# Normalised mLSTM heads turned by VectorE and two DMAs instead of TensorE

## What is computed

```python
num = jnp.einsum('bhts,bhsd->bhtd', s, v) + inter[..., None] * jnp.einsum('bhvd,bhtd->bhtv', C, q)
den = jnp.sum(s, axis=-1) + inter * jnp.einsum('bhd,bhtd->bht', n, q)
h = num / jnp.maximum(jnp.abs(den), jnp.exp(-m_t))[..., None]
...
hm = hm * lax.rsqrt(jnp.mean(hm * hm, axis=-1, keepdims=True) + EPS)
mlstm_out = hm.reshape(B, S, D_MLSTM) * mh_norm_g[l] * o_gate * jax.nn.silu(z_mlstm)
mix = jnp.concatenate([pool_out, mlstm_out], axis=-1)
x = x + gate[:, None, :] * (mix @ w_out[l])
```

## Time and profile before

| | us |
|---|---|
| time, median of 3 runs (1849.15 to 1852.01) | 1849.21 |
| the profiled execution, its own time | 1848.88 |
| its span in the profile | 1847.1 |
| PE busy | 1809.6 |
| VectorE busy | 1013.3 |
| ScalarE busy | 521.5 |

### The profile page before, as it was taken

How to read it: one execution, slowest core, us unless ns; L and a number is a source line. 1 busy time by engine, 2 the same in 40 slices (tenths; PEclk the granted TensorE clock), 3 DMA queues, 4 the chain that set the end, 5 groups by cost and what they waited for, 6 DMA issues and landing times.

```text
span 1847.1 us, 25117 instructions
## 1 busy us (share of the span) xinstructions
PE 1809.6 (98%) x9537; PEld 1554.0 (84%) x9537; DVE 1013.3 (55%) x2247; ACT 521.5 (28%) x1054; POOL 262.1 (14%) x229
## 2 busy tenths in 40 slices
PE   6989999999999999999999999999999999999998
PEld 5878889888898888988888888888889888898886
DVE  6685684527736276353863357452673627735383
ACT  3344331332323132222222223132222313222221
POOL 3433222040210003000030001200022000300000
PEclk9899999999999999999999999999999999999999
DMA  9896735595256552665427653466535665266431
GB/s 329 272 313 181 239 116 181 165 327 194 93 189 194 191 186 85 211 203 178 155 91 242 203 193 104 163 204 216 179 99 189 187 198 189 78 212 202 150 124 69
DMA packets 144348, 336.85 MB, mean 182 GB/s; under 512 B 13068, under 2 KB 55012, under 8 KB 144228
## 3 DMA queue, kind: packets, MB, share of 16 engines
q1 hardware_dynamic: 129028, 312.56, 50.9%
q10 hardware_dynamic: 15200, 22.68, 4.1%
HBM read 288.86 MB, written 46.33 MB: 181 GB/s over the span
## 4 chain that ended last, share of the span: by engine, by line
PE 88%; DVE 7%; issue 2%; ACT 1%; DMA 1%; SPq 0%; POOL 0%; ACTq 0%; DVEq 0%; POOLq 0%
PE ps_acc L511 23%; PE ps_acc L513 23%; PE ps_acc L512 23%; PE ps_kv L511 2%; PE ps_kv L512 2%; PE ps_kv L513 2%; PE ps_num L728 1%; PE ps_kv L732 1%; PE ps_num L727 1%; PE ps_sco L708 1%; PE ps_num L524 1%; PE ps_num L511 1%; PE ps_num L513 1%; PE ps_num L512 1%; PE ps_bro L740 1%
## 5 line engine op out<-in xcount | busy, mean ns | idle before, releaser
L511 PE MATMUL ps_acc<-sb_hT_hi,sb_w_split 128*128 128x512 f32 x1536 | 608.9, 396 | 0.7 <-POOL sb_w_split L1104 0.7
L513 PE MATMUL ps_acc<-sb_hT_hi,sb_w_split 128*128 128x512 f32 x1536 | 599.6, 390 | 0.0
L512 PE MATMUL ps_acc<-sb_hT_lo,sb_w_split 128*128 128x512 f32 x1536 | 598.5, 390 | 0.0
L513 PEld LDWEIGHTS ps_acc<-sb_hT_hi,sb_w_split 128*128 128x128 f32 x1536 | 288.5, 188 | 62.1
L511 PEld LDWEIGHTS ps_acc<-sb_hT_hi,sb_w_split 128*128 128x128 f32 x1536 | 289.0, 188 | 58.5 <-POOL sb_w_split L1104 0.8
L512 PEld LDWEIGHTS ps_acc<-sb_hT_lo,sb_w_split 128*128 128x128 f32 x1536 | 289.1, 188 | 56.9
L1116 POOL TENSOR_TENSOR sb_h_rs<-sb_h_var,sb_mhalf 128x4 f32<-128x4 f32 x32 | 32.4, 1013 | 1019.1 <-DVE sb_h_var L1546 1019.1
L1104 POOL TENSOR_TENSOR sb_w_split<-sb_w_raw,sb_w_split 128x512 fp32r<-128x512 f32 (+1 forms) x64 | 89.0, 1400 | 183.4 <-ACT sb_w_split L812 183.3
L1454 DVE SCALAR_TENSOR_TENSOR sb_acc_cv<-sb_shifted,sb_par,sb_acc_cv 128x512 f32<-128x512 f32 x96 | 76.9, 801 | 60.8 <-ACT sb_acc_cv L964 58.3
L1480 DVE TENSOR_TENSOR sb_oz<-sb_tanh,sb_oz 128x512 f32<-128x512 f32 x32 | 22.2, 692 | 150.5 <-ACT sb_tanh L980 150.5
L511 PE MATMUL ps_acc<-sb_wo_hi,sb_mixm_hi 128*128 128x512 f32 x256 | 103.3, 404 | 0.0
(11 more groups left out here) (219 smaller groups left out, 2867.9 us busy)
## 6 DMA issues: line engine op xcount, KB each, us to landing
sb_w_split<-w_kept SPq DMA_DIRECT2D x328, 512.0 KB, 4.0
sb_w_split<-w_kept SPq DMA_DIRECT2D x56, 520.0 KB, 4.8
w_kept<-sb_w_split SPq DMA_DIRECT2D x40, 512.0 KB, 6.1
sb_x_res<-x SPq DMA_DIRECT2D x34, 512.0 KB, 5.5
sb_w_raw<-w_in SPq DMA_DIRECT2D x64, 256.0 KB, 5.1
out<-sb_qT SPq DMA_DIRECT2D x32, 512.0 KB, 2.9
sb_x_in<-x SPq DMA_DIRECT2D x30, 512.0 KB, 5.8
sb_ada_raw<-w_ada SPq DMA_DIRECT2D x8, 1024.0 KB, 9.6
```

The costliest lines, as they stand in the source:

```text
L511: pe.matmul(dst, st_hi, mv_hi, start=start, stop=False)
L512: pe.matmul(dst, st_hi, mv_lo, start=False, stop=False)
L513: return pe.matmul(dst, st_lo, mv_hi, start=False, stop=stop)
```

## The change

The 128 PE transposes of the heads go. In their place VectorE transposes 32x32 squares of `hm` (`head_turn`, one instruction for the four heads of a chunk), writing into `kT[:, j]`, the place of the keys of that chunk, which are no longer needed by then. ScalarE's queue stores that 256 KB to DRAM (`keep_hm`) and, once it has landed, reads it back with the squares exchanged (`load_hm`: four DMAs for the four groups of 32 channels, each 512 pieces of 128 bytes). `m_mixed` then takes the turned heads from `kT` in SBUF instead of the PSUM bank `bro`. So that one chunk of keys is one contiguous piece, `kT` is laid out by chunk, and the four key tiles are written into it with a stride.

`m_mixed(0)` and `m_mixed(1)` move from the end of iterations 1 and 2 to iterations 2 and 3, right behind `update_c`; `m_mixed(3)` moves from i = 1 to i = 2 of the output stage. `head_turn(j-1)` stands behind `k_w` of iteration j, and `head_turn(3)` behind `head_norm(3)`.

```diff
-        qT, kT, oz = sb("qT", [P, NH, BLK]), sb("kT", [P, NH, BLK]), sb("oz", [P, NH, BLK])
+        qT, kT, oz = sb("qT", [P, NH, BLK]), sb("kT", [P, NC, NH, P]), sb("oz", [P, NH, BLK])
+        hm_kept = nc.dram_tensor("hm_kept", [2, P, BLK], F32, kind="Internal").ap()
...
-                def hm_transposed(j):
-                    bro_wait(5 + j)
-                    pe.wait_ge(hm_ready, b * NC + (j + 1))
-                    for h in range(NH):
-                        last = pe.transpose(bro[:, chunk(h)], hm[:, h, :], ident)
-                    last.then_inc(bro_full, 1)
...
                     tile("zp", j)
-                    if j > 0:
-                        hm_transposed(j - 1)
                     numerator_and_update(j)
...
-                    if i == 1:
-                        hm_transposed(3)
...
+                def keep_hm(j):
+                    act.wait_ge(hm_turned, b * NC + (j + 1))
+                    act.dma_start(hm_kept[j % 2].rearrange("p (h n) -> p h n", h=NH), kT[:, j, :, :]).then_inc(hm_kept_done, 16)
+
+                def load_hm(j):
+                    act.wait_ge(hm_kept_done, 16 * (b * NC + (j + 1)))
+                    squares = hm_kept[j % 2].rearrange("(t c) (h d r) -> c h t d r", c=32, h=NH, r=32)
+                    for d in range(4):
+                        dst = kT[32 * d:32 * d + 32, j, :, :].rearrange("c h (t r) -> c h t r", r=32)
+                        act.dma_start(dst, squares[:, :, :, d, :]).then_inc(hm_loaded, 16)
...
+                    if j > 0:
+                        keep_hm(j - 1)
                     src, free = acc_wait("zp", j)
                     act.wait_ge(q_in_ready, b * NC + (j + 1))
                     if j < NC - 1:
                         load_inter_row(j + 1)
                     tanh_wait(16 + j)
                     act.activation(tanh[:, :], src[:, :], ACT.Tanh, scale=0.5).then_inc(tanh_ready, 1)
+                    if j > 0:
+                        load_hm(j - 1)
...
                 squares(3)
+                keep_hm(3)
                 for i in range(8):
...
+                    if i == 0:
+                        load_hm(3)
...
+                def head_turn(j):
+                    in_turn()
+                    V.transpose(kT[:, j, :, :], hm[:, :, :]).then_inc(hm_turned, 1)
+                    did(hm_turned, b * NC + (j + 1))
...
-                    bro_read(5 + j)
-                    V.tensor_tensor(oz[:, :, chunk(j)], bro[:, :].rearrange("p (h t) -> p h t", t=P), oz[:, :, chunk(j)],
-                                    ALU.mult).then_inc(bro_free, 1)
+                    dve.wait_ge(hm_loaded, 64 * (b * NC + (j + 1)))
+                    V.tensor_tensor(oz[:, :, chunk(j)], kT[:, j, :, :], oz[:, :, chunk(j)], ALU.mult).then_inc(hm_mixed, 1)
...
                         update_c(j - 1)
+                    if j > 1:
+                        m_mixed(j - 2)
...
                     if j > 0:
+                        head_turn(j - 1)
                         y_low(j - 1)
```

More of the change, by code:

```diff
@@ L62 @@
 S_USES = 1 + SCO_FULLS
-B_USES = 9
+B_USES = 5
 SLOT = 1152
@@ L247, in build @@
         y_ready = sem("y_ready")
+        hm_turned, hm_kept_done, hm_loaded, hm_mixed = (
+            sem("hm_turned"), sem("hm_kept_done"), sem("hm_loaded"), sem("hm_mixed"))
         bro_full, bro_free = sem("bro_full"), sem("bro_free")
@@ L309, in chunk, with by_chunk @@
             return slice(P * j, P * j + P)
+        def by_chunk(t):
+            return t.rearrange("p (c t) -> p c t", t=P)
         def col(t, n, m=P):
@@ L707, in heads_to_scores @@
                     for h in range(NH):
-                        last = pe.matmul(sco[:, chunk(h)], kT[:, h, chunk(j)], qT[:, h, chunk(j)], start=True, stop=True)
+                        last = pe.matmul(sco[:, chunk(h)], kT[:, j, h, :], qT[:, h, chunk(j)], start=True, stop=True)
                     last.then_inc(sco_full, 1)
@@ L715, in keys_transposed @@
                     for h in range(NH):
-                        last = pe.transpose(kv[1][:, chunk(h)], kT[:, h, chunk(j)], ident)
+                        last = pe.transpose(kv[1][:, chunk(h)], kT[:, j, h, :], ident)
                     last.then_inc(k_T, 1)
@@ L1654, in one_block @@
                     y_mixed(j)
-                    if 0 < j < 3:
-                        m_mixed(j - 1)
                     if j == 2 and not last_block:
@@ L1694, in one_block @@
                 head_norm(3)
+                head_turn(3)
                 if not last_block:
@@ L1707, in one_block @@
                         out_var(i // 2)
-                    if i == 1:
-                        m_mixed(3)
                     if i in (1, 3):
                         m_low(2 + i // 2)
+                    if i == 2:
+                        m_mixed(3)
                     if i in (1, 3) and not last_block:
```

12 lines of the change are left out of this document (8 added, 4 removed).

## The result

The changed kernel takes 1902.94 us (median; 1900.32 to 1907.27), the kernel before 1849.18 in the same comparison: ratio 1.029, 95% interval 1.027 to 1.031. It is 54 us slower. The forecast was 1859 (1843 to 1879): the sign was right and the size was not. The profiled execution took 1907.27 us, its span is 1905.5.

A forecast was written before the change was run, and what follows sets the result against it. PE was taken as the bound, busy 98% of the span and 88% of the chain. 1848.88 less 2.0 us net gain plus 12 us of new wait gave 1858.9, median forecast 1859, range 1843 to 1879.

The forecast's parts named there:

- VectorE's backlog: VectorE, busy from chunk-loop iteration 2 to the first residual, absorbs most of PE's gain; sum -2.0 us over eight blocks.
- Transposes on PE: Ahead of three numerators and in the output stage: removing them wins at most 1.67 us a block, 13.4 us.
- The turning at 0.69 us: VectorE's `head_turn`, one instruction on 512 f32 columns: 0.69 us, 0.72 with the gap; bounds 0.38 and 1.4.
- Rival 2: VectorE's turning is cheap, 0.38 us, and the loads land in time: -9 us, 1840; chance 0.12.
- four places: PE waits for VectorE at keys of chunk 3, numerator 3, `prep_next(0)` and `out_m(2)`; slacks 1.44 to 2.41 us.
- ScalarE's DMA issues at nothing: ScalarE's five DMA issues per chunk, 2.2 us, fit in its 5 us of idle time ahead of the squares.
- The new wait: VectorE at `m_mixed(0)` waits for the loads of the turned heads: 1.5 us a block, 12 us in all.
- The high end of 4.7 us: Upper case of the wait at `m_mixed(0)`: store 4.7 us, loads one after another, latency and crowding, data at 891.9.
- Price of the wait: Each us `m_mixed(0)` waits is a us of PE, once about 0.5 us left at chunk 3's keys is gone.
- 1: Rival: loads land in time, the rest as forecast; no wait 1847, with up to 0.7 us of wait 1853; chance 0.18.
- 3: Rival: DMA engines pay for pieces, not bytes; a wait of 3.1 us, 25 us in all: 1872; chance 0.15.
- 4: Rival: PE is held by something else, such as weights late behind 65,000 new packets; left inside the range, no separate chance.

## Why the prediction was right and wrong

The time rose by 54 us where 10 were forecast. The terms that failed add up to the 44 between: the wait for the turned heads (34 us, 12 taken), ScalarE's DMA issues (18 for the trip when nobody waits, 16 of it chunk 3's in the output stage; nothing taken), and VectorE's backlog (+2, -2 taken).

- **Transposes on PE:** 1.67 us a block and 13.4 in all; measured 1.64 a block and 12.2 in all. Right.
- **The turning at 0.69 us:** all 32 took 0.711 to 0.715. Right, at the pitch of 0.72 to 0.74 that was used. The Trainium skill's 311 ns for a 128x128 bf16 transpose (VectorE: DVE Perf Modes, The three transpose paths), an estimate of 1.24 us for four, does not carry over to one instruction of 128x512 f32. Rival 2 fell too, which wanted 0.38.
- **VectorE's backlog:** forecast -2.0 us against before, measured +2.1. The stretch and the mechanism were right, the list of places was not. It left out `out_m(1)`, which starts at 918.46 before the change, 1.37 us behind the end of `silu_zp` (917.09). With PE 1.32 us earlier and VectorE 1.44 later that is a wait of 1.4: the 1.37 us of the run without the trip. I looked for gaps at four places and not at each accumulator that VectorE frees. Three of the ordinary blocks therefore gained 0.1 us, not 0.42, the others lost up to 1.1, and block 0 lost 3.2, not 1.6.
- **ScalarE's DMA issues at nothing:** wrong, 16 us. The step looked at ScalarE ahead of the squares in the chunk loop, where the trips did cost only 1.6 us for three chunks. Chunk 3's trip is in the output stage, and there ScalarE works without a gap from `hT_hi` to `m_high(2)`. "Chunk 3 more" was said of the slack of the data, never of the queue.
- **The new wait, 1.5 us a block, 12 us:** wrong, 35 us at chunk 0 and 2.1 at chunk 1. The place was right: it is `m_mixed` of chunk 0, in every block. The terms were mis-sized, in block 3: the store 4.9 us (4.0 taken; 4.6 to 6.9 in the other blocks), the four issues 4.0 us from first to last (1.8 taken, from a DMA of large pieces; 2.6 where nothing disturbs them), the last landing from 2.4 to 9.1 (3.9 taken). The high end of 4.7 us held for blocks 1, 2, 6 and 7 and was passed in four.
- **The error behind them:** I read the DMA share of the kernel before after 885, and saw engines at rest, but the store comes at 879 and runs beside the residual loads and weights that were issued just ahead; in the changed kernel the weights stand 0.3 us ahead of it in seven of the eight blocks. And a late trip meets the next weights, at 885 to 890, which the rows at rest hid.
- **Price of the wait:** one us of PE for each us of VectorE, and that held (47.1 us for 46.4), though by a sum that I had not made: PE's slack takes 3 us of 5.6, and the clock and the later waits give it back.
- **Rivals.** 1 fell: the loads did not land in time. 3 was nearer in size, 3.1 us a block, and half right in kind: the pieces cost 26 us, by way of issue and landing; the engines' own time rose by only 0.7 us a chunk. 4, weights late behind the packets, did not show in the changed kernel; PE waited for no weight.
- **Signs.** As forecast: the wait for `kT` at chunk 0, PE's waits at the turned keys and for `x_res`, the turning's length. Not as forecast: the short waits for `kT` at chunk 1 of three blocks; no wait at L524, since PE loses that time at `out_m(1)` just ahead of it; and PE's busy time rose by 8 us instead of falling by 13, beside a lower clock behind its waits (0.985 in the mean, 0.994 before); where those waits were absent it fell by 13.5 (1796.1 us with neither turning nor trip).

## What to carry to other kernels

A trip through DRAM is store landing, issues and load landing in series; count it at the place where the other queue has just issued its own large DMAs, and follow the queue's own engine through every stage in which it issues, since one chunk here cost ten times as much as the other three together. When work moves to an engine that is behind, list every buffer that it frees for the bound engine, one by one, before claiming what is won. A transpose taken off PE is worth its time only where VectorE's extra instruction falls into idle time: here one chunk in four.

## What the runs showed of the hardware

- One VectorE transpose in 32x32 squares of 128x512 f32 takes 0.711 us, as a one-pass operation of that size does.
- On ScalarE's queue a load of 512 pieces took 0.56 us to issue at least and 0.66 in the median, one of 32 larger pieces with the same bytes 0.31 and 0.44, and a store of 128 pieces 0.33. The longest issue of 512 pieces, 1.66 us, fell in a stretch with the DMA engines 49% busy, so full engines don't explain it. Four such loads held ScalarE for 2.6 to 4.0 us.
- The same store of 256 KB landed after 2.0 us with nothing else under way, after 4.2 to 5.3 us with 512 KB of weights issued on the other queue 0.3 us ahead of it, and after 4.8 to 6.9 us with two residual loads of 512 KB, issued some 3 us ahead, besides.
- A GpSimd subtraction of 128x512 stretched VectorE's operation on two SBUF inputs beside it from 0.69 to 1.67 us.
- 2.5 to 2.8 us of idle PE were followed by 4 us with a mean granted clock of 0.57 to 0.62, most of it at the lower level.
